# A third ready product at the change of stages, GpSimd's share of the statistics, and the row sums of attention on VectorE

## The chip, the cores and the metric

The kernel runs on one core of a Trainium2 chip. The metric is the device time of one execution in microseconds (us). The engines are named in full here; in rows of the profile PE is TensorE, DVE VectorE, ACT ScalarE, POOL GpSimd and SP SyncE, which issues most transfers.

## What is computed

One layer for 2048 tokens of 1024 channels in fp32: a normalization, one wide projection, a pooling branch and a causal stick-breaking attention branch, each with a SiLU gate path, merged by two sigmoid gates, projected out, added to the input and normalized again.

```python
h = rms_norm(x, norm_g)
u_pool, z_pool, q, k, v, z_attn, gate_logits = split(h @ w_in)
y_pool = multiscale_pool(u_pool, pool_w, pool_scale) * silu(z_pool)   # causal means of 2, 4, 8, 16
log_beta     = log_sigmoid(q @ k.T / 8)                               # 8 heads of 64
log_1m_beta  = where(s < t, log_sigmoid(-logits), 0)
later        = reversed_cumsum(log_1m_beta) - log_1m_beta
attn         = where(s < t, exp(log_beta + later), 0) @ v
y_attn = attn * silu(z_attn)
gates  = sigmoid(gate_logits + b_gate)
x = x + (gates[0] * (y_pool @ w_pool_up) + gates[1] * (y_attn @ w_attn_up)) @ w_out
out = rms_norm(x, final_g)
```

## The kernel before

**Products.** Every fp32 product is made of three matmuls on operands split into a high part, rounded to fp32r, and a low remainder (split3, L75 to L77, in the attention stage L1870 to L1874). ScalarE writes the high part ("hi"), GpSimd or VectorE the low one. The large projections go by seven products in place of eight: of the 2 x 2 blocks of a group the products A11, A12, S2, S1, S3, S4 and A22 are formed. These seven are the "parts" of a group, of 12 matmuls of 128x512 each; a part with sums needs an operand that VectorE or GpSimd forms (raw_forms and form_low on the side of the tokens, w_formed on the side of the weights). The results of a group come from sums of parts: ScalarE takes A11, S2 and S1 out of PSUM (take, L1027 in the front, L1983 in attention), VectorE adds A12, S3 and S4 (add_part, L2069), and the four results (A12, S3, S4, A22) are split or activated and stored.

**Three blocks of code.** `front` computes the statistics of the tokens, the normalized and transposed tokens hT, the value projection of 16 token tiles (project_v, L1352 to L1371) and 12 groups of projections, in two halves of 8 tiles and 6 groups. The second half overwrites tiles of the first, so the change of halves waits for stores. `stage3` is the attention stage: 8 heads of 40 items each (an item is up to 128x512 scores), with the remaining projections as filler matmuls between them. `stage4` computes the up projections, gates, output and last normalization. Between the blocks all engines meet at a barrier, and SyncE comes to it when the last stores of the block are done.

**The front.** Each engine's program is written out by hand in the order of slots `s`; PART_AT says which part a slot holds, and functions such as results_at, pooling_at_slot and splits_at say what else an engine does in it. The statistics of tokens go in batches: ScalarE sums squares (square, L951), VectorE makes the mean and its reciprocal (mean, L1149, L1151), ScalarE the square root (root, L956), VectorE refines it to the factors (factors, L1159 to L1165), ScalarE puts a tile's factors on a diagonal (make_diag, L962), TensorE spreads that over the partitions (spread, L1340, into PSUM), and VectorE scales the transposed tokens by it (scale, L1182, eight instructions). ScalarE then rounds them (tile_high, L987) and GpSimd makes the low part (tile_low, through the helper at L871). results_at gives the slot in which the results of a part are split and stored (result_high, L1039); a result of K or Q goes through the tile front_store, which must have been stored before it is written again (SyncE issues the stores, L749). pooled_high (L1055) rounds the level sums of the pooling branch.

**The change of stages.** Two parts of the first group of stage 3 (A11, A12; READY_PARTS) are computed at the end of the front, so that TensorE has work while other engines come to the barrier. Behind it GpSimd fills the tile floor (L2160, L2162), for which VectorE waits before its first instruction.

**Attention.** The items of a head go through rows of 128 queries from the last to the first, and through 1 to 4 blocks of keys in each row. In a slot s ScalarE writes keep (a sigmoid of the scores, L1956), VectorE scans it (scan: L2042 for the first item of a row, L2045 for the others) into left, TensorE turns that (L1901), ScalarE rounds it to wt (L1963) and VectorE makes its low part (L2051), and TensorE multiplies by the values (L1913), with high and low parts of the values side by side. A row's end has four steps: ScalarE copies a half (half_sum, L1971), VectorE adds the other and the end term (add_halves, L2060, into row_sum), and GpSimd adds the two halves into y_out (finish_row, L2103), which VectorE must see done before it writes row_sum two rows on. There are 128 row ends. A head's last twelve items hold eight of them. GpSimd's other work there is the low parts and forms of weights (low_w). The fillers follow a table `due`, which is worked out from a cost per item and gives the number of matmuls that shall be done by each item; the ends of parts follow from it (fin, PART_END, RESULT), and the reload of the second half's forms (hT from form_scratch) from fin as well. A result k is activated by ScalarE (result), and for z strips multiplied by VectorE (silu, L2073); the result with k % 4 = 3 goes to sum_d, straight from PSUM, so that the filler behind it, which needs that bank, waits for it.

```python
fin = [-1] * READY_PARTS + [next(s for s in range(len(due)) if due[s] >= ends_at[r]) for r in range(READY_PARTS, PARTS)]
PART_END = [f + 1 for f in fin]
RESULT = [fin[result_part(k)] + 1 for k in range(RESULTS)]
```

## Time and profile before

| | |
|---|---|
| three runs | 1577.16, 1579.95, 1581.51 us; median 1579.95 |
| profiled execution | 1579.27 us |
| its span, first to last instruction | 1577.4 us |
| mean granted TensorE clock | 0.992 |
| HBM read, written | 166.80 MB, 85.99 MB (160 GB/s over the span) |

The busy shares stand in the first group of rows below. TensorE is busy nearly everywhere, so the profile is best read by what ends its idle times (the list of waits), by windows around them with the granted clock, and by the timelines of the engines that end them. Busy time of TensorE counts an instruction from its start to a modelled end, and neighbouring matmuls overlap.

### The profile page before, as it was taken

The page shows a single profiled execution, that of the slowest core. Times are in us where ns is not written, and L with a number is a line of the kernel's source. Part 1 is how long each engine was busy: PE and PEld are TensorE (multiplying, and loading weights), DVE is VectorE, ACT ScalarE, POOL GpSimd, SP SyncE. Part 2 cuts the span into 40 slices and gives each one's busy share as a digit, 9 for nine tenths or more (in the row PEclk, how much of TensorE's full clock was granted, in tenths as well). Part 3 has the DMA queues.
Part 4 walks back from the last instruction along what each step waited for, and adds up shares of the span by engine and source line. Part 5 has one row for each costly group of instructions (what it writes and reads, how often), then busy time and mean ns, then how long its engine had stood idle before and what let it go on. Part 6 is the DMA issues. An engine that isn't in the chain of part 4 may idle for free. (4 is left out here: it accounts for less than half of the span.)

```text
span 1577.4 us, 24982 instructions
## 1 busy us (share of the span) xinstructions
PE 1530.4 (97%) x7770; PEld 1275.2 (81%) x7770; DVE 1237.2 (78%) x1592; ACT 856.2 (54%) x1653; POOL 1102.0 (70%) x770
## 2 busy tenths in 40 slices
PE   7999999998999999999998999999999999999998
PEld 5787878886888887888877888888888788888886
DVE  7968595766987788887897887798878656687987
ACT  6546554444666665666665676666766512233342
POOL 4899876985977678777766776787756334456774
PEclk9999999999999999999999999999999999999999
DMA  7468942465344343343694442443423688764552
GB/s 270 151 240 310 376 125 92 118 214 169 87 109 112 89 127 102 94 139 93 185 329 143 129 120 87 120 114 99 121 71 83 209 272 257 251 197 166 181 190 110
DMA packets 170803, 254.45 MB, mean 161 GB/s; under 512 B 48417, under 2 KB 82209, under 8 KB 170674
## 3 DMA queue, kind: packets, MB, share of 16 engines
q1 hardware_dynamic: 170674, 252.85, 51.2%
q8 instruction: 66, 1.08, 0.3%
q14 instruction: 63, 0.52, 0.1%
HBM read 166.80 MB, written 85.99 MB: 160 GB/s over the span
## 5 line engine op out<-in xcount | busy, mean ns | idle before, releaser
L2103 POOL TENSOR_TENSOR ring<-raw,ring 128x512 fp32r<-128x512 f32 x140 | 241.2, 1723 | 154.3 <-ACT ring L1950 143.9
L2045 DVE TENSOR_TENSOR_SCAN left<-keep,left 128x512 f32<-128x512 f32 x192 | 283.8, 1478 | 61.9 <-issue 40.1
L1870 PE MATMUL psum<-hT,ring 128*128 128x512 f32 x664 | 273.9, 412 | 14.7 <-ACT sum_a L1983 5.1
L1874 PE MATMUL psum<-hT,ring 128*128 128x512 f32 x664 | 271.8, 409 | 0.0
L1872 PE MATMUL psum<-hT,ring 128*128 128x512 f32 x664 | 271.2, 408 | 0.0
L1956 ACT ACTIVATE keep<-psum 128x512 f32<-128x512 f32 (+3 forms) x320 | 170.8, 534 | 131.8 <-PE psum L1893 119.2
L1963 ACT ACTIVATE wt<-psum 128x512 fp32r<-128x512 f32 (+3 forms) x320 | 171.0, 534 | 111.3 <-PE psum L1901 108.6
L2051 DVE TENSOR_TENSOR wt<-psum,wt 128x512 fp32r<-128x512 f32 (+3 forms) x320 | 190.3, 595 | 16.5 <-ACT wt L1963 13.9
L1913 PEld LDWEIGHTS psum<-wt,vm 128*128 128x128 f32 x1088 | 171.6, 189 | 26.9 <-DVE wt L2051 1.5
L1913 PE MATMUL psum<-wt,vm 128*128 128x256 f32 x1088 | 181.5, 281 | 1.0 <-DVE wt L2051 1.0
L1901 PE MATMUL psum<-ident,left 128*128 128x128 f32 x1088 | 171.1, 272 | 4.0 <-DVE wt L2051 4.0
L1901 PEld LDWEIGHTS psum<-ident,left 128*128 128x128 f32 x1088 | 137.2, 141 | 44.7 <-DVE left L2042 2.7
L2042 DVE TENSOR_TENSOR_SCAN left<-keep,floor 128x512 f32<-128x512 f32 (+3 forms) x128 | 134.7, 1052 | 32.4 <-ACT keep L1956 30.6
L1870 PEld LDWEIGHTS psum<-hT,ring 128*128 128x128 f32 x664 | 126.3, 190 | 37.1 <-DVE sum_d L2073 6.3
L1874 PEld LDWEIGHTS psum<-hT,ring 128*128 128x128 f32 x664 | 126.2, 190 | 18.6
L1872 PEld LDWEIGHTS psum<-hT,ring 128*128 128x128 f32 x664 | 126.4, 190 | 17.6
L871 POOL TENSOR_TENSOR ring<-raw,ring 128x512 fp32r<-128x512 f32 x76 | 120.9, 1591 | 27.6 <-ACT ring L1049 18.6
L75 PE MATMUL psum<-hT,ring 128*128 128x512 f32 x344 | 134.6, 391 | 3.4 <-POOL ring L871 1.5
L77 PE MATMUL psum<-hT,ring 128*128 128x512 f32 x344 | 134.1, 390 | 0.0
L76 PE MATMUL psum<-hT,ring 128*128 128x512 f32 x344 | 134.1, 390 | 0.0
L2103 POOL TENSOR_TENSOR y_out<-row_sum 64x128 f32<-64x128 f32 x128 | 101.0, 789 | 42.8 <-DVE row_sum L2060 27.9
L1892 PE MATMUL psum<-km,qm 128*128 128x512 f32 (+3 forms) x320 | 116.2, 363 | 2.9 <-DMA qm<-qk_scratch 2.1
(262 smaller groups left out, 3410.1 us busy)
## 6 DMA issues: line engine op xcount, KB each, us to landing
raw<-in_w_strips SPq DMA_DIRECT2D x144, 256.0 KB, 4.0
qm<-qk_scratch SPq DMA_DIRECT2D x128, 128.0 KB, 4.5
gate<-gate_scratch SPq DMA_DIRECT2D x64, 256.0 KB, 4.7
form_scratch<-hT SPq DMA_DIRECT2D x28, 512.0 KB, 7.0
hT<-form_scratch SPq DMA_DIRECT2D x28, 512.0 KB, 8.3
km<-qk_scratch SPq DMA_DIRECT2D x64, 128.0 KB, 3.7
merged_scratch<-rows SPq DMA_DIRECT2D x32, 256.0 KB, 5.0
mt<-merged_scratch SPq DMA_DIRECT2D x16, 512.0 KB, 5.8
```

The costliest lines, as they stand in the source:

```text
L75: pe.matmul(out, w_hi, m_hi, start=start, stop=False, skip_group_check=onto)
L1870: pe.matmul(o, hi, m_hi, start=k == 0 and not onto, stop=False, skip_group_check=onto)
L1872: pe.matmul(o, hi, m_lo, start=False, stop=False, skip_group_check=onto)
L1874: last = pe.matmul(o, lo, m_hi, start=False, stop=k == HK - 1, skip_group_check=onto)
L1901: last = pe.transpose(bank_t(n)[:, j * P:(j + 1) * P], left[:, n % LN, a:a + P], ident[:, :])
L1913: last = pe.matmul(bank_o(row), vm[:, t % VN, j, :], wt[:, n % WN, j, :, :].rearrange("p a q -> p (a q)"), start=first and j == 0, stop=fi ...
L1956: act.activation(keep[:, n % 2, CH - w:CH], bank_s(n)[:, 0:w], ACT.Sigmoid, scale=-SCALE).then_inc(keep_done, 1)
L1963: act.activation(wt[:, n % WN, 0:w // P, 0, :], bank_t(n)[:, 0:w].rearrange("p (j q) -> p j q", q=P), ACT.Copy).then_inc(wt_hi_done, 1)
L2042: dve.tensor_tensor_scan(left[:, n % LN, span][:, ::-1], k, floor[:, span][:, ::-1], carry, ALU.mult, ALU.max).then_inc(scanned, 1)
L2045: dve.tensor_tensor_scan(left[:, n % LN, span][:, ::-1], k, k, carry, ALU.mult, ALU.bypass).then_inc(scanned, 1)
L2051: dve.tensor_tensor(wt[:, n % WN, 0:w // P, 1, :], bank_t(n)[:, 0:w].rearrange("p (j q) -> p j q", q=P), wt[:, n % WN, 0:w // P, 0, :].bit ...
L2103: pool.tensor_tensor(out_, a, b, op).then_inc(s, 1)
```

## The change

1. `READY_PARTS` goes from 2 to 3. The front computes a third product (S2) of stage 3's first group, and ScalarE takes A11's product there, into a tile `ready_sum` that is handed to stage 3 as sum_a. Stage 3's fillers begin with S1, and 1980 matmuls of them are left of 1992, so that the table `due` gives other steps.
2. The factors of batches 2, 3, 4 and 5 are worked out by GpSimd. VectorE's mean(4) moves from before the loop of slots into tile_step(2), ScalarE's rounding of tile 2 moves ahead of root(3), and mean(b) waits for the factors of the batch before.
3. In results_at the last group of either half (groups 5 and 11) has its results one slot sooner; before, this held for the very last part alone. pooled_high comes one slot later, and there ahead of the splits.
4. In attention VectorE does finish_row, behind the scan of the same slot, and GpSimd no longer does. ScalarE's and VectorE's part of every fourth result comes ahead of the keep, or the row's end and scan, of its slot.

Calls that only pass `ready_sum` on, and the assertion that results stay in order, are left out here.

```diff
@@ -273,8 +273,9 @@
         head_loads = HeadLoads(sem, heads, qk_d, v_d)
+        ready_sum = heads("sum_a", [P, CH])[:, :]
         front(nc, sem, psum, at, free_at, hT_at, ident, ident_r, gcol, bcol, pscol, v_ends, hT, ring, raws, staging, ring_at, raw1_at,
-              x, x_T, norm_gT, w_v, b_gateT, pool_scaleT, w_strips, pool_w, pool_fix, v_d, qk_d, mix_d, form_d, head_loads)
+              x, x_T, norm_gT, w_v, b_gateT, pool_scaleT, w_strips, pool_w, pool_fix, v_d, qk_d, mix_d, form_d, head_loads, ready_sum)
...
@@ -295,7 +296,7 @@
 FRONT_PARTS = FRONT_GROUPS * FORMS
-READY_PARTS = 2
+READY_PARTS = 3
 RING_AT = FRONT_PARTS % RING
...
@@ -548,8 +549,8 @@
         lagged = [PART_AT.get(s - 2), PART_AT.get(s - 1)]
-        at_slot = [r for r, last in zip(lagged, (False, True))
-                   if r is not None and r < FRONT_PARTS and (r == FRONT_PARTS - 1) == last]
+        at_slot = [r for r, soon in zip(lagged, (False, True))
+                   if r is not None and r < FRONT_PARTS and (r // FORMS % HALF_GROUPS == HALF_GROUPS - 1) == soon]
         return [(r // FORMS, r % FORMS) for r in at_slot if not is_u(r // FORMS) and r % FORMS in OUT_PARTS]
...
@@ -891,6 +892,22 @@
+            def factors(b):
+                tiles = range(*BATCHES[b])
+                pool.wait_ge(rooted, b + 1)
+                for n in tiles:
+                    last = pool.tensor_scalar(stat[:, 4, n:n + 1], stat[:, 3, n:n + 1], stat[:, 3, n:n + 1],
+                                              stat[:, 1, n:n + 1], ALU.mult, ALU.mult)
+                last.then_inc(statistics, 1)
+                pool.wait_ge(statistics, 5 * b + 3)
+                part = stat[:, 5, tiles.start:tiles.stop]
+                pool.tensor_scalar(part, stat[:, 4, tiles.start:tiles.stop], -0.5, 1.5, ALU.mult, ALU.add).then_inc(statistics, 1)
+                pool.wait_ge(statistics, 5 * b + 4)
+                for n in tiles:
+                    last = pool.tensor_scalar(stat[:, 6, n:n + 1], stat[:, 5, n:n + 1], stat[:, 3, n:n + 1], 1.0,
+                                              ALU.mult, ALU.mult)
+                last.then_inc(statistics, 1)
+
...
@@ -909,6 +926,10 @@
                 i = n % FRONT_TILES
+                if n == 2:
+                    factors(4)
+                if batch_at(n) is not None:
+                    factors(batch_at(n))
                 if i in (3, 5):
...
@@ -926,7 +947,9 @@
                      wv_lo_pool, i - WV // 2 + 1)
+            factors(2)
             tile_low(1)
+            factors(3)
             for s in range(SLOTS):
...
@@ -1001,7 +1024,8 @@
                 i = n % FRONT_TILES
-                tile_high(n)
+                if n != 2:
+                    tile_high(n)
                 if later(n):
...
@@ -1024,7 +1048,10 @@
                     act.wait_ge(summed, 3 * (g - 1) + FRONT_ADD[S3 if j == A11 else S4])
-                act.activation(sum_u if j == S2 else sum_a, bank(g, j), ACT.Copy).then_inc(taken, 1)
+                if g == FRONT_GROUPS:
+                    act.wait_ge(mixed, 2 * MIXED_FIRST)
+                act.activation(ready_sum if g == FRONT_GROUPS else sum_u if j == S2 else sum_a, bank(g, j), ACT.Copy
+                               ).then_inc(taken, 1)
...
@@ -1085,6 +1112,7 @@
             square(3)
+            tile_high(2)
             root(3)
...
@@ -1092,7 +1120,7 @@
                 r = PART_AT.get(s - 1)
-                if r is not None and r < FRONT_PARTS:
+                if r is not None and r <= FRONT_PARTS:
                     g, j = divmod(r, FORMS)
...
@@ -1106,6 +1134,9 @@
                     copy_v(n - 2)
+                for f, q, step in pooling_at_slot(s):
+                    if step == LEVELS[q] + 2:
+                        pooled_high(f, q)
                 for w in splits_at(s):
...
@@ -1117,9 +1148,6 @@
                         mix_weights_high(f)
-                for f, q, step in pooling_at_slot(s):
-                    if step == LEVELS[q] + 1:
-                        pooled_high(f, q)
                 for f, q in mixes_at(s - 1):
...
@@ -1145,6 +1173,8 @@
                 tiles = slice(*BATCHES[b])
+                if b:
+                    dve.wait_ge(statistics, 5 * b)
                 dve.wait_ge(squared, BATCHES[b][1])
...
@@ -1153,7 +1183,7 @@
                 dve.wait_ge(rooted, b + 1)
-                if tiles.stop - tiles.start <= 2:
+                if tiles.stop - tiles.start == 1:
                     root_of = [stat[:, 3, n:n + 1] for n in range(tiles.start, tiles.stop)]
...
@@ -1209,7 +1239,9 @@
                 i = n % FRONT_TILES
-                if n != 2:
+                if n == 2:
+                    mean(4)
+                else:
                     scale(n)
...
@@ -1218,7 +1250,6 @@
                     mean(batch_at(n))
-                    factors(batch_at(n))
...
@@ -1289,13 +1320,9 @@
             mean(2)
-            factors(2)
             first_forms(0)
             mean(3)
-            factors(3)
             scale(2)
-            mean(4)
-            factors(4)
             for s in range(SLOTS + 2):
...
@@ -2001,13 +2029,17 @@
             act.sem_inc(w_hi_done, RING)
+            act.sem_inc(taken, 1)
             for s in range(-9, END):
...
                     for j in TAKE:
-                        if s == PART_END[part(g, j)]:
+                        if s == PART_END[part(g, j)] and part(g, j) > 0:
                             take(g, j)
+                for k in at(RESULT, s):
+                    if k % 4 == 3:
+                        result(k)
                 if 0 <= s < ALL:
...
@@ -2018,7 +2050,8 @@
                 for k in at(RESULT, s):
-                    result(k)
+                    if k % 4 < 3:
+                        result(k)
                 if ALL - 4 <= s < ALL:
...
@@ -2060,6 +2093,16 @@
+            def finish_row(n):
+                e, i, row = item(n)[0], item(n)[1], row_of(n)
+                mine = slice(e * HD, e * HD + HD)
+                u = row // 4
+                dve.wait_ge(row_done, row + 1)
+                if i % 4 == 3:
+                    wait(dve, y_stored[u % 2], u // 2, DMA)
+                dve.tensor_tensor(y_out[mine, u % 2, i % 4 * P:i % 4 * P + P], row_sum[mine, row % 2, 0:P],
+                                  row_sum[mine, row % 2, P:2 * P], ALU.add).then_inc(y_done, 1)
+
...
@@ -2080,12 +2123,17 @@
                             add_part(g, j)
+                for k in at(RESULT, s):
+                    if kind(k // 4) < 2 and k % 4 == 3:
+                        silu(k)
                 if s - AV_LAG - 1 in LAST:
...
                     scan(s)
+                if s - AV_LAG - 1 in LAST:
+                    finish_row(s - AV_LAG - 1)
                 for k in at(RESULT, s):
-                    if kind(k // 4) < 2:
+                    if kind(k // 4) < 2 and k % 4 < 3:
                         silu(k)
...
@@ -2121,16 +2169,6 @@
-            def finish_row(n):
-                e, i, row = item(n)[0], item(n)[1], row_of(n)
-                mine = slice(e * HD, e * HD + HD)
-                u = row // 4
-                pool.wait_ge(row_done, row + 1)
-                if i % 4 == 3:
-                    wait(pool, y_stored[u % 2], u // 2, DMA)
-                step(y_out[mine, u % 2, i % 4 * P:i % 4 * P + P], row_sum[mine, row % 2, 0:P],
-                     row_sum[mine, row % 2, P:2 * P], ALU.add, y_done, row + 1)
-
...
@@ -2171,8 +2209,6 @@
                         value_lo(u)
-                if s - AV_LAG - 1 in LAST:
-                    finish_row(s - AV_LAG - 1)
                 for k in at(RESULT, s):
...
                         times_mix(k)
```

**ScalarE at the start of the front.** The names: stat holds the statistics (L956 root, before; L979 after), diag the diagonals, xt_ring and xt_first the tokens whose squares are summed, hT<-xT the rounding of a tile. Before:

```order
L956 ACTIVATE stat<-stat 128x1 [waits f_statistics]
L962 ACTIVATE diag<-ident,stat 128x128 [waits f_spread,f_statistics]
L951 ACTIVATE xt_first,stat<-xt_first 128x1024 [waits f_x_in0]
L951 ACTIVATE xt_first,stat<-xt_first 128x1024 [waits f_x_in1]
L956 ACTIVATE stat<-stat 128x2 [waits f_statistics]
L987 ACTIVATE hT<-xT 128x4x128 [waits f_scaled] x2
L962 ACTIVATE diag<-ident,stat 128x128 [waits f_spread,f_statistics]
L951 ACTIVATE xt_ring,stat<-xt_ring 128x1024 [waits f_x_in2]
```

and with the change:

```order
L1010 ACTIVATE hT<-xT 128x4x128 [waits f_scaled] x2
L979 ACTIVATE stat<-stat 128x1 [waits f_statistics]
L985 ACTIVATE diag<-ident,stat 128x128 [waits f_spread,f_statistics]
L974 ACTIVATE xt_first,stat<-xt_first 128x1024 [waits f_x_in0]
L974 ACTIVATE xt_first,stat<-xt_first 128x1024 [waits f_x_in1]
L979 ACTIVATE stat<-stat 128x2 [waits f_statistics]
L985 ACTIVATE diag<-ident,stat 128x128 [waits f_spread,f_statistics]
L974 ACTIVATE xt_ring,stat<-xt_ring 128x1024 [waits f_x_in2]
```

The two roundings of tile 2 stood behind two squares and a root; now they stand ahead of root(3), and the diagonal, the squares and root(4) behind them.

**ScalarE at the change of halves**, in the last group of the first half. front_store<-... is the high part of a result, wv_hi a split of the value weights for the second half, front_sum_u and front_sum_a takes, ring the high part of filler weights. Before:

```order
L1039 ACTIVATE front_store<-psum 128x512 [waits f_out_lo,f_hi_stored2,f_part]
L970 ACTIVATE wv_hi<-wv_raw 128x1024 [waits f_wv_in1]
L1049 ACTIVATE ring<-raw_6_65 128x512 [waits f_part,f_block_in1]
L970 ACTIVATE wv_hi<-wv_raw 128x1024 [waits f_wv_in2]
L1027 ACTIVATE front_sum_u<-psum 128x512 [waits f_summed,f_part]
L1049 ACTIVATE ring<-raw_0_58 128x512 [waits f_part,f_block_in0]
L1039 ACTIVATE front_store<-front_out_d 128x512 [waits f_out_lo,f_hi_stored0,f_summed]
L970 ACTIVATE wv_hi<-wv_raw 128x1024 [waits f_wv_in3]
L962 ACTIVATE diag<-ident,stat 128x128 [waits f_spread,f_statistics] x2
```

and with the change:

```order
L1066 ACTIVATE front_store<-psum 128x512 [waits f_out_lo,f_hi_stored2,f_part]
L993 ACTIVATE wv_hi<-wv_raw 128x1024 [waits f_wv_in1]
L1076 ACTIVATE ring<-raw_6_65 128x512 [waits f_part,f_block_in1]
L1066 ACTIVATE front_store<-front_out_d 128x512 [waits f_out_lo,f_hi_stored0,f_summed]
L993 ACTIVATE wv_hi<-wv_raw 128x1024 [waits f_wv_in2]
L1053 ACTIVATE front_sum_u<-psum 128x512 [waits f_summed,f_part]
L1076 ACTIVATE ring<-raw_0_58 128x512 [waits f_part,f_block_in0]
L993 ACTIVATE wv_hi<-wv_raw 128x1024 [waits f_wv_in3]
L985 ACTIVATE diag<-ident,stat 128x128 [waits f_spread,f_statistics] x2
```

The result from front_out_d stands three places sooner and ahead of the take of front_sum_u.

**VectorE at two row ends of attention.** left is written by the scans, wt by the low parts, row_sum by add_halves. Before:

```order
L2060 SCALAR_TENSOR_TENSOR row_sum<-psum,v_ends,half_sum 64x256 [waits s3_y,s3_half]
L2042 SCALAR_TENSOR_TENSOR left<-keep,floor 128x128 [waits s3_turned,s3_keep]
L2051 TENSOR_TENSOR wt<-psum,wt 128x2x128 [waits s3_wt_hi]
L2045 SCALAR_TENSOR_TENSOR left<-keep,left 128x512 [waits s3_turned,s3_keep,s3_scanned]
L2051 TENSOR_TENSOR wt<-psum,wt 128x4x128 [waits s3_wt_hi]
L2060 SCALAR_TENSOR_TENSOR row_sum<-psum,v_ends,half_sum 64x256 [waits s3_y,s3_half]
```

and with the change:

```order
L2093 SCALAR_TENSOR_TENSOR row_sum<-psum,v_ends,half_sum 64x256 [waits s3_y,s3_half]
L2075 SCALAR_TENSOR_TENSOR left<-keep,floor 128x128 [waits s3_turned,s3_keep]
L2103 TENSOR_TENSOR y_out<-row_sum 64x128 [waits s3_y_stored0,s3_row]
L2084 TENSOR_TENSOR wt<-psum,wt 128x2x128 [waits s3_wt_hi]
L2078 SCALAR_TENSOR_TENSOR left<-keep,left 128x512 [waits s3_turned,s3_keep,s3_scanned]
L2084 TENSOR_TENSOR wt<-psum,wt 128x4x128 [waits s3_wt_hi]
L2093 SCALAR_TENSOR_TENSOR row_sum<-psum,v_ends,half_sum 64x256 [waits s3_y,s3_half]
```

Between the scan and the low part behind it VectorE now adds the row's halves into y_out.

## Rows read from the trace of the kernel before

**Rows 1.** The page, part 1: busy us, share of span, instructions by engine.

```profile
PE 1530.4 (97%) x7770; PEld 1275.2 (81%) x7770; DVE 1237.2 (78%) x1592; ACT 856.2 (54%) x1653; POOL 1102.0 (70%) x770
```

**Rows 2.** TensorE's waits: line, what ended them, total us, times, longest.

```profile
PE psum L1870 <- ACT sum_a L1983: 5.1, 1, 5.1
PE psum L1870 <- DVE sum_d L2073: 4.2, 4, 1.7
PE psum L1901 <- DVE wt L2051: 4.0, 4, 2.3
PE psum L1870 <- DMA hT<-form_scratch: 3.9, 1, 3.9
PE psum L1352 <- ACT hT L987: 2.7, 1, 2.7
PE psum L75 <- ACT front_sum_u L1027: 1.4, 1, 1.4
```

**Rows 3.** Windows: stretch, length, TensorE busy (instructions), granted clock, DMA share, GB/s.

```profile
25.00:30.00 5.00, 2.20 (x7) 0.74 0.26 107
373.40:376.00 2.60, 2.57 (x6) 0.50 0.41 101
834.40:838.00 3.60, 3.60 (x11) 0.50 1.03 337
607.00:612.00 5.00, 2.72 (x16) 1.00 0.02 3
```

**Rows 4.** Timeline (start, us), TensorE, end of the front; 35 alike between.

```profile
359.81 0.39 PE L77 MATMUL psum<-hT,ring 128*128 128x512 f32 x1
...
367.97 0.39 PE L77 MATMUL psum<-hT,ring 128*128 128x512 f32 x1
```

**Rows 5.** Timelines, start of the front; in brackets idle before, releaser.

```profile
27.68 1.13 ACT L987 ACTIVATE hT<-xT 128x512 fp32r<-128x512 f32 x2
...
30.22 0.63 PE L1340 MATMUL psum<-diag,ones 128*128 128x128 f32 x2
...
35.92 1.19 PE L1352 MATMUL psum<-wv_hi,b 128*128 128x512 f32 x4 [0.69 <-ACT b L987]
```

**Rows 6.** Timelines of ScalarE and TensorE, around the change of halves.

```profile
181.36 0.60 ACT L1027 ACTIVATE front_sum_u<-psum 128x512 f32<-128x512 f32 x1 [1.08 <-PE psum L77]
...
183.88 0.39 PE L75 MATMUL psum<-hT,ring 128*128 128x512 f32 x1
...
185.29 0.63 ACT L1039 ACTIVATE front_store<-front_out_d 128x512 fp32r<-128x512 f32 x1 [2.82 <-issue]
...
199.49 1.16 PE L1352 MATMUL psum<-wv_hi,b 128*128 128x512 f32 x4 [1.87 <-ACT b L987]
```

**Rows 7.** Timelines of GpSimd and VectorE, at the change of stages.

```profile
372.77 0.52 POOL L2160 MEMSET floor<- 128x512 f32 x1 [7.74 <-POOLq L682]
...
373.76 0.69 DVE L2069 TENSOR_TENSOR sum_b<-psum,sum_a 128x512 f32<-128x512 f32 x1 [5.55 <-POOL floor L2162]
```

**Rows 8.** Groups by line in the attention stage (VectorE), and the page's of GpSimd.

```profile
L2045 DVE TENSOR_TENSOR_SCAN left<-keep,left 128x512 f32<-128x512 f32 x192 | 283.8, 1478 | 61.9 <-issue 40.1 <-ACT keep L1956 20.1 <-PE psum L1901 0.7
...
L2060 DVE SCALAR_TENSOR_TENSOR row_sum<-psum,v_ends,half_sum 64x256 f32<-64x256 f32 x128 | 61.5, 481 | 25.1 <-POOL y_out L2103 11.9 <-ACT half_sum L1971 11.4
...
L2073 DVE TENSOR_TENSOR sum_b<-sum_b,staging 128x512 f32<-128x512 f32 x8 | 11.6, 1445 | 1.8 <-ACT staging L1998 1.7
...
L2103 POOL TENSOR_TENSOR y_out<-row_sum 64x128 f32<-64x128 f32 x128 | 101.0, 789 | 42.8 <-DVE row_sum L2060 27.9
```

**Rows 9.** Timeline of VectorE, an add of 128x256 from SBUF in the front.

```profile
341.81 0.42 DVE L123 TENSOR_TENSOR v_raw<-v_prev,v_raw 128x256 f32<-128x256 f32 x1
```

**Rows 10.** Windows of all engines, sum over the eight stretches with eight row ends.

```profile
sum 216.80, PE 213.85 PEld 182.61 DVE 183.25 ACT 154.32 POOL 149.50; mean PE 26.73 PEld 22.83 DVE 22.91 ACT 19.29 POOL 18.69
```

**Rows 11.** Timelines of VectorE and TensorE, a scan and the matmuls that turn it.

```profile
480.19 0.69 DVE L2042 TENSOR_TENSOR_SCAN left<-keep,floor 128x256 f32<-128x256 f32 x1 [0.42 <-ACT keep L1956]
...
483.52 0.38 PE L1901 MATMUL psum<-ident,left 128*128 128x128 f32 x2
```

9 lines of the change are left out of this document (5 added, 4 removed).

## Prediction

> **What bounds the kernel now.** I read the share of each engine first. The profiled execution took 1579.27 us. TensorE is busy 97% of the span and VectorE 78% [rows 1], so time is won only where TensorE stands idle or runs at half its clock, and lost where something new stops it. TensorE's list of waits names the places that the change touches [rows 2]: 5.1 us for ScalarE's first sum of the attention stage (the change of stages), 4.2 us for the SiLU of sum_d, 4.0 us for wt, 3.9 us for a reloaded form, 2.7 us for hT at the start, 1.4 us for front_sum_u. The windows add what an idle costs behind it [rows 3]: after the idle of 5.1 us the granted clock was 0.50 (1.2 GHz, against 1.00 for 2.4 GHz), it was 0.50 after the reload's 3.9 us, and it had begun to fall at the start, behind the 2.7 us. Behind the idle of 2.3 us at 607 it stayed at 1.00. From 359.81 to 367.97 TensorE goes 36 steps from one matmul to the next [rows 4], 0.227 us each, so 12 of them take 2.72 us. At the half clock 6 fill 2.57 us [rows 3], 0.43 each. A stay there as long as the reload's 3.6 us or more [rows 3] loses at least half of itself; from the durations between the two levels I take 2.7 to 3.4 us for a clock fall beyond the idle.
>
> **The start of the front.** The factors of statistics batches 2 to 5 go to GpSimd, and ScalarE rounds tile 2 before root(3), where it did so behind root(4). Removed: the wait for hT. That work ended at 28.8 and was queued behind two squares and a root [rows 5]; now it follows the scaling directly, and the first product can start near 27.6, 0.75 us sooner. Added: diag(3), the two squares, mean(4) and root(4) are all later by the 1.13 us rounding and the wait for its input. I place the squares' end at 29.5 and root(4) at 30.2. GpSimd's five small operations follow, each waiting for the one before. No row shows one on GpSimd; its fill of 128x512 took 0.52 us [rows 7], so each costs between nothing and 0.52. I take 0.34 with its hand-over, since one column is far less work than a fill: 1.7 us for five, so diag(4) is ready near 32.4. The spread matmul that stood at 30.22 without a wait [rows 5] then waits until there, TensorE's queue behind it. The next scaling follows, and the product that started at 35.92 starts near 37.8: +1.9, taken as **+2**. Bounds: −1 (the five at almost nothing, the start's clock kept) to +4.5 (0.52 us each and a longer stay at the half clock). Batches 2, 3 and 5 stay beside VectorE's scalings, which they relieve.
>
> **Pooled levels behind the takes.** pooled_high one slot later but ahead of the splits frees ScalarE for front_sum_u. The 1.4 us wait goes [rows 2]: **−1.4**.
>
> **The change of halves.** Group 5's results now come one slot sooner, so the result of S4 (front_store from front_out_d) stands ahead of a weight split and of the take of front_sum_u on ScalarE. The take began at 181.36; that result could only start at 185.29 after 2.82 us of waiting for a store to land [rows 6]. Now ScalarE stands from some 179.3 until that landing, which nothing makes earlier, and the split and the take follow it: the take at 186.6, done at 187.2. TensorE's part that needs the emptied bank began at 183.88 without a wait [rows 6]: a stall of 3.3 us. Of it 1.9 us come back, as the wait of 1.87 us at 199.49 for the next store's landing [rows 6] ends no later, and some 0.9 as the last results leave a slot sooner: +0.5. But 3.3 us lies above the 2.7 us behind which the clock fell [rows 3], which adds 2.7: **+3**. Bounds +0.5 and +3.2.
>
> **The change of stages.** TensorE ended at 368.36 [rows 4] and idled for 5.1 us, to 373.4 [rows 2]. ScalarE's take of A11, and GpSimd's fill of the floor, from 372.77, both stood behind the barrier, and VectorE's first add behind the floor [rows 7]. The barrier waits for the last results' stores. Now TensorE has 12 more matmuls, to 371.1 (2.72 us), and the last group's three other results leave one slot sooner, so I open the barrier 0.8 us sooner. The third part's A11 product is taken in the front; what then holds TensorE is VectorE's add of A12, behind the floor: 371.9 + 1.75 = 373.6. It restarts as late as before with 12 matmuls fewer to do: −2.7, +0.2: −2.5. The idle is 2.5 us in place of 5.1, in between 2.3 (no fall) and 2.7 (fall); without the fall another −2.6. I take half: **−3.8**, bounds −1.7 (the barrier no sooner) and −5.1.
>
> **The attention stage.** Off GpSimd go 128 sums of a row's halves, 789 ns each, 101 us [rows 8]; onto VectorE come 128 of the same shape, 64x128 from SBUF. VectorE waited 11.9 us in row_sum for GpSimd's sums [rows 8]; TensorE's stall of 2.3 us, most of the 4.0 for wt, hangs on one of these. ScalarE's and VectorE's part of every fourth result moves ahead of the keep and scan of its slot: that is TensorE's wait for sum_d, 4.2 us [rows 2]. Together some 6 us can be won. What does a sum cost on VectorE? From adds of 128x512 (0.69) and 128x256 (0.42) [rows 7, 9] a line gives 0.28 at 128 columns. The SiLU products, which read SBUF twice, took 1.45 us into sum_b [rows 8], and scans of 512 average 1.48 [rows 8], their spread coming, as I read it, from GpSimd's products beside them. So a sum costs 0.28 to 1.45; I take 0.8, a little under the middle, as it is the shortest operation and GpSimd, now the idler, meets fewer of them: 102 us more on VectorE. The cover: one stretch of some 27 us in each of the eight heads has eight row ends; in these, VectorE is idle 33.6 of 216.8 us in all [rows 10]. 64 sums at 0.8 are 51 us; relief from GpSimd, a third less busy there, I put at 5 us over all scans. 51 − 34 − 5 = 12 us short, 1.5 per stretch, against a lead of 2.6 us from a scan (ended 480.88) to the matmul that turns it (483.52) [rows 11]. It is carried, with some 2 us of new small stalls: **−4**, bounds −6 and the rival below.
>
> The Trainium skill, page "SBUF — State Buffer", section "SBUF: two separate sides", speaks against this move: a VectorE operation with two SBUF inputs and a GpSimd one that reads SBUF exclude each other, and the loser waits for the other's whole instruction. By it a sum would cost up to 0.28 plus one GpSimd product of 1.7 us, and the stage would lose rather than gain; the products and scans here agree in kind.
>
> **The reload at 834.40.** The steps move by one part, and the form loads' issue moves some 1.5 us sooner, as GpSimd sheds sums ahead of its last use; but one index later by the due table. 3.9 us of idle and a clock fall stand there [rows 2, 3]. **−1**, bounds −7 (both gone) and +3.
>
> Sum: +2 −1.4 +3 −3.8 −4 −1 = −5.2: 1574.1 for the profiled execution. The median of the runs is 1579.95, 0.7 above it: **1574.7**.
>
> **The rivals.**
> *New waits in front, clock falling.* The start at +4.5, the halves at +3.2, the stage change at −2.5 with its clock fall kept, attention −2, the reload 0: +1.8, 1581.8. For it: each of the three idles lies near 2.7, and the spread matmul had no wait. Against: the start's price rests on operations that may be short. 0.24.
> *VectorE becomes the bound (slower).* The mechanism is the sum in the eight dense stretches at 1.2 us, midway from 0.94 (below) to the SiLU product's 1.45: 77 − 34 − 5 = 38 us short, 4.7 a stretch, 2.6 of it carried, 2.1 times 8 = +17 where I have −4: 1574.7 + 21 = 1596. It decides from a mean of (34 + 5 + 21)/64 = 0.94 us. Between 0.8 and this point the small stalls grow, and the time runs from 1575 to 1580. Against: GpSimd also loses 101 us of the work that would stand in the way. 0.14.
> *More of the idles vanish.* The start −1, halves +0.5, stage change −5.1, attention −5, reload −4, pooled −1.4: −16.0, 1564. For it: each clock fall is all or nothing. 0.15.
> *It does not do what it says.* If the barrier is opened by a store or by TensorE itself, the third product only fills the idle: that is in the stage change's bound of −1.7 (within my case, 1577).
>
> **How the numbers follow.** My forecast has 0.47, with 1570 to 1579 as its own range. About 0.3%, 4.7 us, can be told from no change: faster is below 1575.2. My case gives 0.34 faster and 0.13 the same; the first rival 0.18 the same and 0.06 slower; the second 0.14 slower; the third 0.15 faster. Faster 0.49, the same 0.31, slower 0.20. The range of 1564 to 1586 reaches to the third case and the first's slower half, and leaves out 0.2, above all the VectorE case.
>
> **What would show it.** The spread matmul at the start waiting for ScalarE's diag some 2 us, and the half clock beyond 34 us. The 1.4 us wait for front_sum_u gone from 142.75, and one of about 3 us on it near 187. At the change of stages an idle of 2.3 to 2.7 ended by VectorE's sum_b, with or without a clock of 0.50. In attention no wait for sum_d above 0.5 us, y_out on VectorE near 0.8 mean, VectorE's sum up by 80 to 110 us, no rise in waits for wt. Wrong it would be if y_out averaged over 1 us and waits for wt grew to 10 us or more, or if the halves cost nothing.

## The result, and the profile after

The changed kernel's median is 1587.23 us (1584.94 to 1589.43, five runs), against 1579.95 for the kernel before (1575.48 to 1581.51). The ratio of the runs is 1.0059, with a 95% interval of 1.0042 to 1.0076. So it is slower, by 7.3 us in the medians and 9.3 by that ratio, where 5 us less were forecast, and it lies outside the range given (1564 to 1586). The profiled execution took 1584.94 us, with a span of 1583.2 us, 5.7 us over the profiled one of before.

TensorE's waits in the changed kernel, in the form of [rows 2]:

```profile
PE psum L1929 <- DVE wt L2084: 12.2, 16, 5.3
PE psum L1367 <- ACT diag L985: 6.0, 3, 3.0
PE psum L75 <- ACT front_sum_u L1053: 3.3, 1, 3.3
PE psum L1898 <- DVE sum_b L2112: 3.0, 1, 3.0
PE psum L1898 <- DMA hT<-form_scratch: 2.7, 2, 2.1
PE psum L1920 <- issue: 2.6, 1, 2.6
PE psum L1898 <- DVE sum_c L2112: 2.5, 2, 1.5
```

The waits of 5.1 us for sum_a, 4.2 us for sum_d, 2.7 us for hT and 1.4 us for front_sum_u are gone, and the one for the reloaded form fell from 3.9 to 2.7 us. In their place stand 6.0 us for the diagonals, 3.3 us for another front_sum_u, 3.0 us for sum_b and, the largest, 12.2 us for wt (5.0 before), with one wait of 5.3 us in it that nothing in the prediction foresaw. All engines over the attention stage (from:to, length, then busy us and instructions of TensorE, its weight loads, VectorE, ScalarE and GpSimd, then clock, DMA share and GB/s), before and after:

```profile
379.00:1240.00 861.00, 843.30 (x4801) 717.27 (x4801) 720.13 (x874) 570.50 (x1133) 629.17 (x458) 1.00 0.43 123
```

```profile
379.00:1240.00 861.00, 840.39 (x4774) 713.62 (x4773) 807.00 (x989) 564.38 (x1124) 553.96 (x331) 0.99 0.42 123
```

VectorE went from 84% to 94% busy there, GpSimd from 73% to 64%.

Where the time went is read best from the same instruction of TensorE in both timelines: its start in the kernel before, and how much later it starts in the changed one (and in three kernels of the next section). Product matmuls of the front are those of L75 to L77. Each column is one execution.

| place | before, us | changed | results alone (e6) | results and row sums (e4) | losses undone (e8) |
|---|---|---|---|---|---|
| 301st product matmul of the front | 138.5 | +2.3 | −0.3 | −0.1 | −0.1 |
| 421st | 167.6 | +0.7 | −2.0 | −1.8 | −1.8 |
| 41st of the second half's values | 205.3 | +3.9 | −1.4 | −1.1 | −0.8 |
| first matmul of scores | 378.7 | +3.4 | −1.1 | −1.4 | −0.7 |
| 17th of scores | 397.9 | +9.1 | −1.3 | −1.4 | +0.8 |
| last of scores | 1230.2 | +4.9 | −6.5 | −2.4 | −2.0 |
| end of the span | 1577.4 | +5.7 | −5.2 | −0.9 | −2.1 |

Behind the 205.3 the changed kernel's lag settles at +3.6 from about 213 to the end of the front. Later figures for other kernels are read in the same way: a lag is the distance from the kernel before at the same instruction. The part behind the 17th scores differs between executions of the same attention code: the kernels e6 and e12 below gain 5.3 and 9.5 us there, the changed kernel, e1 and e2 4.2, 3.5 and 0.3, and e3 loses 0.6.

**Start.** ScalarE, TensorE and GpSimd of the changed kernel, which answer to [rows 5]:

```profile
27.10 0.40 ACT L985 ACTIVATE diag<-ident,stat 128x128 f32<-128x128 f32 x1 [1.12 <-POOL stat L907]
...
32.60 0.40 ACT L985 ACTIVATE diag<-ident,stat 128x128 f32<-128x128 f32 x1 [2.31 <-POOL stat L907]
...
30.40 1.29 POOL L899 TENSOR_SCALAR stat<-stat 128x1 f32<-128x1 f32 x2 [0.68 <-ACT stat L979]
31.78 0.19 POOL L904 TENSOR_SCALAR stat<-stat 128x2 f32<-128x2 f32 x1
32.07 0.49 POOL L907 TENSOR_SCALAR stat<-stat 128x1 f32<-128x1 f32 x2
...
27.56 0.80 PE L1367 MATMUL psum<-diag,ones 128*128 128x128 f32 x2 [2.39 <-ACT diag L985]
...
33.05 0.80 PE L1367 MATMUL psum<-diag,ones 128*128 128x128 f32 x2 [2.99 <-ACT diag L985]
```

GpSimd's five operations take 2.2 us, and diag(4) starts at 32.60. TensorE waits twice, for diag(3) and for diag(4), with its clock at 0.50 from 26.9 to 37.1 us, where it was 27.4 to 34.2 before.

**The change of halves.** In the form of [rows 6]:

```profile
185.91 0.63 ACT L1066 ACTIVATE front_store<-front_out_d 128x512 fp32r<-128x512 f32 x1 [5.91 <-DMA qk_scratch<-front_store]
186.45 1.04 ACT L993 ACTIVATE wv_hi<-wv_raw 128x1024 fp32r<-128x1024 f32 x1
187.39 0.58 ACT L1053 ACTIVATE front_sum_u<-psum 128x512 f32<-128x512 f32 x1
...
188.02 0.79 PE L75 MATMUL psum<-hT,ring 128*128 128x512 f32 x1 [3.31 <-ACT front_sum_u L1053]
```

ScalarE stands 5.9 us for a store to land, and what is queued behind it reaches TensorE as a stall of 3.3 us. (The row of before, in [rows 6], put its 2.82 us down to "issue"; this one names the store.) The window behind it shows the half clock, as do windows behind the change of stages, the opening of attention and the reload:

```profile
188.00:191.00 3.00, 2.98 (x7) 0.50 1.04 412
378.30:381.60 3.30, 3.30 (x10) 0.52 0.33 85
395.80:398.60 2.80, 2.80 (x11) 0.50 0.41 89
842.50:845.80 3.30, 3.30 (x13) 0.53 1.04 323
```

**The change of stages.** GpSimd, VectorE and TensorE, in the form of [rows 7]:

```profile
375.88 0.53 POOL L2198 MEMSET floor<- 128x512 f32 x1 [6.90 <-POOLq L683]
...
376.88 0.69 DVE L2112 TENSOR_TENSOR sum_b<-psum,sum_a 128x512 f32<-128x512 f32 x1 [5.53 <-POOL floor L2200]
...
377.62 0.50 PE L1898 MATMUL psum<-hT,ring 128*128 128x512 f32 x1 [2.96 <-DVE sum_b L2112]
```

TensorE now waits 2.96 us for VectorE's add, which stands behind the floor.

**The opening of attention.** Here the largest single loss arises. ScalarE, GpSimd, VectorE and TensorE of the changed kernel:

```profile
386.79 0.61 ACT L1984 ACTIVATE keep<-psum 128x512 f32<-128x512 f32 x1
391.72 0.63 ACT L1978 ACTIVATE ring<-second 128x512 fp32r<-128x512 f32 x1 [4.33 <-POOL second L2151]
392.25 0.58 ACT L1991 ACTIVATE wt<-psum 128x512 fp32r<-128x512 f32 x1
392.73 0.62 ACT L2026 ACTIVATE staging<-sum_c 128x512 f32<-128x512 f32 x1
...
389.62 2.06 POOL L2151 TENSOR_TENSOR second<-raw,raw 128x512 f32<-128x512 f32 x1
...
393.38 1.60 DVE L2116 TENSOR_TENSOR sum_c<-sum_c,staging 128x512 f32<-128x512 f32 x1 [2.75 <-ACT staging L2026]
394.91 0.68 DVE L2084 TENSOR_TENSOR wt<-psum,wt 128x512 fp32r<-128x512 f32 x1
...
395.74 1.09 PE L1929 MATMUL psum<-ident,left 128*128 128x128 f32 x4 [5.29 <-DVE wt L2084]
```

and ScalarE in the kernel before:

```profile
384.50 0.62 ACT L1963 ACTIVATE wt<-psum 128x512 fp32r<-128x512 f32 x1
...
390.67 0.62 ACT L1950 ACTIVATE ring<-second 128x512 fp32r<-128x512 f32 x1
391.31 0.60 ACT L1963 ACTIVATE wt<-psum 128x512 fp32r<-128x512 f32 x1
```

`second` is the S2 operand of the second filler group, which GpSimd forms behind two low parts and another form. Its split by ScalarE (ring<-second) stood ahead of the fourth wt before, and met an operand that was ready; now it stands ahead of the first. With a third product taken out of the stage, TensorE is 12 matmuls further on at the same item, the parts end at earlier items, and the split moves with them: ScalarE comes to it 4.3 us too early, and the first wt, at 384.50 before, waits until 392.25 behind it.

**Row sums.** y_out in the changed kernel (count, duration ns min/median/max), VectorE's groups of the attention stage in the form of [rows 8], and the sum over the eight stretches with eight row ends in the form of [rows 10]:

```profile
L2103 DVE TENSOR_TENSOR y_out<-row_sum x128: 254/760/1365, 409.1 to 1246.5; 64x128 f32<-64x128 f32 x128
```

```profile
L2078 DVE TENSOR_TENSOR_SCAN left<-keep,left 128x512 f32<-128x512 f32 x192 | 282.9, 1473 | 18.7 <-issue 12.3 <-ACT keep L1984 5.3 <-PE psum L1929 0.2
...
L2103 DVE TENSOR_TENSOR y_out<-row_sum 64x128 f32<-64x128 f32 x128 | 104.6, 817 | 2.0
```

```profile
sum 216.80, PE 213.01 PEld 180.99 DVE 206.60 ACT 150.39 POOL 120.82; mean PE 26.63 PEld 22.62 DVE 25.83 ACT 18.80 POOL 15.10
```

A sum costs 0.82 us, as estimated, and VectorE is left with 10 us of idle in 217 us where it had 34. The scans of this line average 1473 ns where they had 1478, but the two kernels differ in more than the sums; e4 and e6 below compare them alone.

### The profile page after: what moved, and what is told of

Its sections match the earlier page's. It is cut to its first block and busy times, and to the rows that moved or that the text cites. A ratio compares the mean times of both kernels' runs of the same rounds, so it can differ in the third digit from the quotient of the medians.

```text
span 1583.2 us, 24892 instructions
## 1 busy us (share of the span) xinstructions
PE 1533.0 (97%) x7770; PEld 1276.5 (81%) x7770; DVE 1321.9 (84%) x1704; ACT 854.6 (54%) x1653; POOL 1032.1 (65%) x658
## 5 line engine op out<-in xcount | busy, mean ns | idle before, releaser
L2151 POOL TENSOR_TENSOR ring<-raw,ring 128x512 fp32r<-128x512 f32 x140 | 251.0, 1793 | 236.5 <-ACT ring L1978 231.0
L2078 DVE TENSOR_TENSOR_SCAN left<-keep,left 128x512 f32<-128x512 f32 x192 | 282.9, 1473 | 18.7 <-issue 12.3
L1929 PE MATMUL psum<-ident,left 128*128 128x128 f32 x1088 | 171.8, 273 | 12.3 <-DVE wt L2084 12.2
L2075 DVE TENSOR_TENSOR_SCAN left<-keep,floor 128x512 f32<-128x512 f32 (+3 forms) x128 | 145.1, 1134 | 13.9 <-ACT keep L1984 12.2
L75 PE MATMUL psum<-hT,ring 128*128 128x512 f32 x348 | 137.3, 395 | 5.0 <-ACT front_sum_u L1053 3.3
L872 POOL TENSOR_TENSOR ring<-raw,ring 128x512 fp32r<-128x512 f32 x76 | 119.7, 1574 | 28.6 <-ACT ring L1076 19.3
L77 PE MATMUL psum<-hT,ring 128*128 128x512 f32 x348 | 136.6, 393 | 0.0
L1920 PE MATMUL psum<-km,qm 128*128 128x512 f32 (+3 forms) x320 | 116.4, 364 | 3.1 <-issue 2.6
L1921 PE MATMUL psum<-km,qm 128*128 128x512 f32 (+3 forms) x320 | 117.1, 366 | 0.0
```

Source lines behind the costliest of these rows:

```text
L75: pe.matmul(out, w_hi, m_hi, start=start, stop=False, skip_group_check=onto)
L77: return pe.matmul(out, w_lo, m_hi, start=False, stop=stop, skip_group_check=onto)
L1929: last = pe.transpose(bank_t(n)[:, j * P:(j + 1) * P], left[:, n % LN, a:a + P], ident[:, :])
L2078: dve.tensor_tensor_scan(left[:, n % LN, span][:, ::-1], k, k, carry, ALU.mult, ALU.bypass).then_inc(scanned, 1)
L2151: pool.tensor_tensor(out_, a, b, op).then_inc(s, 1)
```

## The experiments

Twelve kernels ran, five executions or more each. The medians of the kernel before beside them were 1579.2 to 1580.0 us. The interval of one kernel's ratio is some 2 us to either side, so a difference between two of them is uncertain by about 3 us, and the timelines of the profiled runs are read beside them. Gains over the changed kernel are given by the medians; by the ratios to the kernel before they are up to 2 us larger, as the changed kernel's own loss is (9.3 in place of 7.3).

**e1: the statistics as before.** From the changed kernel, GpSimd's factors are taken out and ScalarE's order at the start is put back:

```diff
             square(3)
-            tile_high(2)
             root(3)
...
             mean(2)
+            factors(2)
             first_forms(0)
             mean(3)
+            factors(3)
             scale(2)
+            mean(4)
+            factors(4)
```

> The changed kernel with the statistics as they were (factors on VectorE, the rounding of tile 2 behind root(4)). Theory 1 (each order puts a wait of its own on TensorE): the two waits for ScalarE's diag, 2.4 and 3.0 us near 27.5 and 33, go, one of 2.7 us for hT comes back, and the product behind stands 2.6 us sooner; later gaps keep their size, so the time is some 2 to 3 us under the changed kernel's. Rival (the start's loss is swallowed by a later wait for a store): the offset at the change of halves is the same as in the changed kernel, and the time stays within 1 us of it.

Measured: 1584.18 us (1582.52 to 1589.58), 3.0 us under the changed kernel. The two waits for diag are gone; the 2.75 us for hT is back, and the first scores stand 2.6 us sooner than in the changed kernel. That is so although this execution lost 1.8 us to the very first diagonal, at 8.8 us, which the change does not touch. Theory 1 holds for the start, with a size at the limit of what the runs can tell.

**e2: the results of group 5 in their old slots.**

```diff
-                   if r is not None and r < FRONT_PARTS and (r // FORMS % HALF_GROUPS == HALF_GROUPS - 1) == soon]
+                   if r is not None and r < FRONT_PARTS and (r // FORMS == FRONT_GROUPS - 1) == soon]
```

> The changed kernel with the results of group 5 in their old slots (those of the last group, 11, stay one slot sooner). Theory 1: ScalarE's take of front_sum_u no longer stands behind the result from front_out_d, so TensorE's wait of 3.3 us near 188 and the half clock of 6.8 us behind it go, the wait of about 1.9 us for b near 200 comes back, and everything behind is 2.9 us sooner: time 2 to 4 us under the changed kernel's. Rival: the old order would wait for the same landing in another place, and nothing is won.

Measured: 1585.98 us (1585.38 to 1588.68), 1.3 us under the changed kernel, less than the 2 to 4 expected and within the uncertainty. In the trace the wait for front_sum_u is gone, one of 2.82 us for b at 201.24 is in its place, and the first scores stand 1.9 us sooner (+1.4 against +3.4). From the 421st product of the front to its end this execution loses 0.6 us where the changed kernel loses 2.9. In the traces of all kernels the old order loses 0.6 to 1.2 us there (e2, e4, e6 to e8, e11, e12) and the new one 1.5 to 3.7 (the changed kernel, e1, e3, e5, e9, e10). So the new order costs, some 2 us, and a part of what pooled_high had gained is waited off in either order, here with 2.82 us for b in place of 1.87.

**e3: wt ahead of the splits in the first ten slots.**

```diff
+                if 0 <= s - T_LAG < 8:
+                    high_part(s - T_LAG)
                 for w in at(W_STEP, s):
                     split_w(w)
-                if 0 <= s - T_LAG < ALL:
+                if 8 <= s - T_LAG < ALL:
                     high_part(s - T_LAG)
```

> The changed kernel, but in the first ten slots of attention ScalarE rounds wt before it splits filler weights. Theory 2 (with three ready products ScalarE's split of the S2 operand comes ahead of the first wt and waits 4.3 us there for GpSimd to form it, and wt, VectorE's low part and TensorE's turn are queued behind): TensorE's stall of 5.3 us near 396 and the half clock near 395 to 399 go or shrink below 1.5 us, offset at the end of attention and time 4 to 6 us less. Rival (VectorE is too busy with what it took over): its order is not touched, so the stall stays above 4 us and the time within 1.5 us.

Measured: 1584.28 us (1582.89 to 1591.99; the profiled execution is the slowest, 1591.99), 3.0 us under the changed kernel. The stall at the opening shrank only from 5.3 to 3.9 us, and from the first to the 17th scores this kernel loses 5.6 us, as much as the changed one (5.7). Theory 2 in this form fell, its rival (a stall above 4 us, the time within 1.5) did not come out either, and no trace locates the 3 us. The trace does say why the stall stayed. ScalarE and VectorE of this kernel:

```profile
387.66 0.61 ACT L1991 ACTIVATE wt<-psum 128x512 fp32r<-128x512 f32 x1
392.12 0.63 ACT L1978 ACTIVATE ring<-second 128x512 fp32r<-128x512 f32 x1 [3.84 <-POOL second L2153]
392.65 0.61 ACT L2026 ACTIVATE staging<-sum_c 128x512 f32<-128x512 f32 x1
...
393.30 0.74 DVE L2118 TENSOR_TENSOR sum_c<-sum_c,staging 128x512 f32<-128x512 f32 x1 [2.27 <-ACT staging L2026]
393.96 0.68 DVE L2086 TENSOR_TENSOR wt<-psum,wt 128x512 fp32r<-128x512 f32 x1
```

wt's high part is early now, at 387.66, but VectorE's low part stands behind the SiLU of sum_c, whose sigmoid (staging) still stands behind ring<-second on ScalarE. The wait was taken out of one of two paths.

**e5: the split itself two slots later.** This takes both away.

```diff
     def split_step(w):
-        return fin[freed(w)] + 1 if w >= RING else -99
+        return fin[freed(w)] + (3 if freed(w) == 4 else 1) if w >= RING else -99
```

> The changed kernel, but the split of the tenth filler part's weights (S2 of the second group, whose operand GpSimd forms at the opening) two slots later, so that neither wt nor the sigmoid for sum_c stands behind ScalarE's wait for it. Theory 2b (the opening's stall is ScalarE's wait for the formed operand, and what is queued behind it on ScalarE and VectorE): the stall of 5.3 us near 396 falls under 1.5 us, no half clock there, and the sixteenth item stands 5 to 6 us sooner against the first than in the changed kernel; time 1580 to 1583. Rival (GpSimd's low parts or VectorE's load are late in any order): the stall stays above 3.5 us, the time above 1584.

Measured: 1583.50 us (1576.86 to 1588.94), 3.7 us under the changed kernel. ScalarE, VectorE and TensorE:

```profile
388.79 0.61 ACT L1991 ACTIVATE wt<-psum 128x512 fp32r<-128x512 f32 x1
...
392.08 1.68 DVE L2116 TENSOR_TENSOR sum_c<-sum_c,staging 128x512 f32<-128x512 f32 x1
393.68 0.68 DVE L2084 TENSOR_TENSOR wt<-psum,wt 128x512 fp32r<-128x512 f32 x1
...
394.51 0.87 PE L1929 MATMUL psum<-ident,left 128*128 128x128 f32 x3 [2.53 <-DVE wt L2084]
```

ScalarE no longer waits ahead of wt, but 2.5 us of the stall are left: VectorE has three scans, two SiLU products and an add ahead of the first low part, where the kernel before had three scans and one SiLU product (its second came at 393.72, behind three low parts). The add and the second product take 2.3 us. So theory 2b accounts for 2.8 of the 5.3 us, and the rest, as I read it, is work of VectorE that the third product pulls into the filling of the pipeline. The rival was right about that rest; neither side's figure for the stall (under 1.5, above 3.5) came out. From the first to the 17th scores the loss is 3.2 us here and 1.5 in e8, which has the same edit, against 5.7 in the changed kernel; with the stall of 5.3 us unchanged it is 6.9 in e1, 6.0 in e2 and 7.0 in e9, where the clock stands at 0.50 for 6.8 us in place of 3.4.

**e10: two ready products.** All else as changed:

```diff
-READY_PARTS = 3
+READY_PARTS = 2
...
-                if r is not None and r <= FRONT_PARTS:
+                if r is not None and r < FRONT_PARTS:
...
-            act.sem_inc(taken, 1)
...
-                        if s == PART_END[part(g, j)] and part(g, j) > 0:
+                        if s == PART_END[part(g, j)]:
```

> The changed kernel with two ready products as before, all else as changed. Theory 2: the opening's stall of 5.3 us and its half clock go, 12 matmuls (2.7 us) come back into the stage and the idle at the change of stages grows by 2 us: 1583 to 1586. If the third product is worth what it was meant to be (an idle filled, no other cost): 1589 or more.

Measured: 1579.98 us (1577.78 to 1583.08), 7.3 us under the changed kernel, more than the 1 to 4 expected. The idle at the change of stages is 4.56 us in place of 2.96, the 12 matmuls are back, and still the last scores stand 5.0 us sooner (−0.1 against +4.9). There is no stall of more than 0.9 us at the opening, and from the first to the 17th scores nothing is lost (−0.2): one constant makes the opening's loss come and go. The third ready product cost as much as the whole change lost, 7.3 us in the medians; that is more than its stall of 5.3 us. By the two profiled executions it is 4.6 us from the front's end to the last scores, and what lies between that and the 7.3 was not located.

**e4, e6, e7: the two moves in attention, apart and together.** All three take the front, the statistics and the two ready products of the kernel before, and keep pooled_high behind the takes. e4 has both moves. e6 has the order of every fourth result alone:

```diff
+                for k in at(RESULT, s):
+                    if k % 4 == 3:
+                        result(k)
                 if 0 <= s < ALL:
                     remaining(s)
...
                 for k in at(RESULT, s):
-                    result(k)
+                    if k % 4 < 3:
+                        result(k)
...
+                for k in at(RESULT, s):
+                    if kind(k // 4) < 2 and k % 4 == 3:
+                        silu(k)
                 if s - AV_LAG - 1 in LAST:
                     add_halves(s - AV_LAG - 1)
...
                 for k in at(RESULT, s):
-                    if kind(k // 4) < 2:
+                    if kind(k // 4) < 2 and k % 4 < 3:
                         silu(k)
```

and e7 has the row sums alone (GpSimd's finish_row goes):

```diff
                 if s < ALL:
                     scan(s)
+                if s - AV_LAG - 1 in LAST:
+                    finish_row(s - AV_LAG - 1)
```

> The kernel before with only the attention part of the change (row sums on VectorE, every fourth result ahead of the keep and scan) and pooled_high behind the takes; two ready products, statistics and results of the front as before. Theory 1 and 2 (the losses lie in the front and at the opening of attention, the moves in attention win): no stall for wt above 2 us at the opening, attention 2 to 5 us shorter than before, time 3 to 6 us under the kernel before. Rival (VectorE is the bound with sums of 0.82 us): waits for wt and sum_c grow to 7 us or more as in the changed kernel, attention is as long as before or longer, time within 1.5 us of before or over it.

> The kernel before with every fourth result ahead of the keep and scan and pooled_high behind the takes, row sums on GpSimd as before. Theory 3 (the order of the results wins, the move of the row sums gives back what it wins): waits for sum_d under 1 us in all in place of 4.2, the 2.3 us wait behind GpSimd's row sum stays; time 2 to 4 us under the kernel before, and at least as low as with the row sums on VectorE (1577.5). Rival (the row sums' move carries the gain): time within 1.5 us of before.

> The kernel before with the row sums on VectorE and pooled_high behind the takes, results in their old order. Theory 3: a sum costs 0.8 us, waits for wt grow by 3 us or more over the 4.0 of before, the 4.2 us for sum_d stay; time between that of before and 3 us over it, or at best 1 us under it for pooled_high. Rival: waits for wt do not grow, the 2.3 us one goes, and the time is 2 us or more under before.

| kernel | results early | row sums | median, us | ratio, 95% interval |
|---|---|---|---|---|
| e6 | yes | GpSimd | 1570.61 | 0.9941 (0.9925 to 0.9958) |
| e4 | yes | VectorE | 1577.45 | 0.9983 (0.9971 to 0.9994) |
| e7 | no | VectorE | 1590.02 | 1.0068 (1.0055 to 1.0082) |

The order of results is worth 9 us with pooled_high's 1.7, and the row sums take 7 of them back (e4 against e6); without the order they cost 11 (e7 against before). The two are not independent: with the row sums on VectorE and the results late, the waits for sum_d do not stay at 4.2 us but grow to 7.1, with one of 3.1. Theory 3 holds, and more strongly than expected: e7 lies 11 us over before where at most 3 was expected, and e6 beat its expected 2 to 4 us. e4 lies between its two cases: the waits grew as the rival said, and the time is 2.5 us under before, where theory had 3 to 6 and the rival 1.5 or less. TensorE's waits, e6, then e4:

```profile
PE psum L1906 <- DVE wt L2060: 4.0, 4, 2.2
PE psum L1918 <- DVE wt L2060: 1.0, 1, 1.0
```

```profile
PE psum L1906 <- DVE wt L2060: 6.1, 11, 1.0
PE psum L1918 <- DVE wt L2060: 3.5, 2, 1.8
```

The eight stretches with eight row ends, e6, then e4:

```profile
sum 216.80, PE 213.80 PEld 182.61 DVE 184.63 ACT 152.21 POOL 148.99; mean PE 26.73 PEld 22.83 DVE 23.08 ACT 19.03 POOL 18.62
```

```profile
sum 216.80, PE 213.63 PEld 181.69 DVE 209.13 ACT 152.87 POOL 115.89; mean PE 26.70 PEld 22.71 DVE 26.14 ACT 19.11 POOL 14.49
```

VectorE stands at 96% in e4's. The waits for wt grow from 5.0 us in 5 places to 9.6 us in 13. The scans do get shorter: all 320 of them take 417.7 us in e4 and 427.4 in e6, and 428.0 in the changed kernel against 442.9 in e9, which has the row sums back on GpSimd. So GpSimd's relief is there, 10 to 15 us, and it does not keep TensorE from waiting more.

**e9: the changed kernel with the row sums back on GpSimd.** Its edit is e7's taken back, with finish_row in GpSimd's loop as before.

> The changed kernel with the row sums on GpSimd as before, all else as changed. Theory 3 (the row sums on VectorE are the largest loss, 7 to 10 us, and hide the gain of the results' order): 1578 to 1581, waits for wt beside the opening's under 3 us, none for sum_c above 0.5. Rival (with three ready products the opening decides, and the row sums cost little there): 1584 or more.

Measured: 1581.95 us (1578.85 to 1583.62), 5.3 us under the changed kernel and just above the expected 1578 to 1581. The opening's stall stays at 5.28 us, and behind it one wait of 0.93 us for wt and one of 0.74 us for sum_c are left. This confirms e4 against e6 from the other side, and the stall at the opening does not come from the row sums.

**e11: a spare sum.** e6's kernel, and on VectorE a sum that nobody needs, into a tile of its own:

```diff
+            def spare_sum(n):
+                e, row = item(n)[0], row_of(n)
+                mine = slice(e * HD, e * HD + HD)
+                dve.wait_ge(row_done, row + 1)
+                dve.tensor_tensor(spare[mine, :], row_sum[mine, row % 2, 0:P - 8],
+                                  row_sum[mine, row % 2, P:2 * P - 8], ALU.add)
...
                 if s < ALL:
                     scan(s)
+                if s - AV_LAG - 1 in LAST:
+                    spare_sum(s - AV_LAG - 1)
```

> The kernel with only the order of results and pooled_high changed (1570.6), row sums on GpSimd, and beside them a spare sum on VectorE: 64x120 of the same two halves behind the same scans, written to a tile nobody reads. It leaves nothing out and adds 128 instructions. Theory 3a (it is VectorE's time that costs, in the dense stretches): the spare sum takes 0.7 to 1.0 us in the mean, TensorE's waits for wt grow as with the row sums there, and the time is 5 to 10 us over 1570.6. Rival (it is the new dependence, y_out's place ahead of the low part and the store's wait, that costs): within 2 us of 1570.6.

Measured: 1590.44 us (1588.61 to 1593.27), 19.8 us over e6. VectorE, GpSimd and the waits:

```profile
L2077 DVE TENSOR_TENSOR spare<-row_sum 64x120 f32<-64x120 f32 x125 | 99.2, 794 | 1.9
...
L2125 POOL TENSOR_TENSOR y_out<-row_sum 64x128 f32<-64x128 f32 x125 | 114.2, 914 | 43.9 <-DVE row_sum L2070 29.6 <-POOL ring L2125 1.5 <-POOL raw L2125 0.8
```

```profile
PE psum L1907 <- DVE wt L2061: 10.5, 12, 2.9
```

No result waits for this sum and no store holds it, so neither the dependence nor the store's wait is needed for a cost, as the rival had it; the place ahead of the low part is the same here, and a sum placed behind it was not tried. The expected 5 to 10 us were far too few. The cost need not be VectorE's time alone: GpSimd's own sum takes 914 ns here against 815 in e6, its products (ring) 1758 against 1718, VectorE's scans 1513 against 1488, and TensorE waits once, for 3.9 us, for GpSimd's vm; time on VectorE and the slowing of both engines were not told apart. With GpSimd's own sums kept beside it the price is 20 us where the move costs 7: by difference, what else the move does (above all the 101 us that GpSimd loses) would be worth some 13 us, an estimate.

**e8: the three losses undone.** The changed kernel with e1's, e2's and e5's edits together.

> The changed kernel with all three losses undone: statistics as before, group 5's results in their old slots, the tenth split two slots later; third ready product, pooled_high, the last group's results, results and row sums of attention as changed. If the ledger adds up (start 2.6, halves 2.9, opening 5.8 us less): 1574 to 1577. If the losses are not independent (a later wait swallows them, or the clock falls elsewhere): 1578 or more.

Measured: 1579.28 us (1576.98 to 1583.65), ratio 0.9999 (0.9988 to 1.0011). With the single gains of e1 (3.0), e2 (1.3) and e5 (3.7) the sum is 1587.3, against 1587.23 measured for the changed kernel: the three are independent as far as the runs can tell. Still the time fell into the case "1578 or more": 1574 to 1577 was added up from the timelines' 2.6, 2.9 and 5.8 us, and the edits gave back 8.0 in all, the opening above all less than its 5.8. Against e4, which has neither the third product nor the last group's results sooner, it is 1.8 us slower, within the uncertainty: even without ScalarE's wait no gain of the third product is seen.

**e12: the rounding of tile 2 between the two squares**, on e6's kernel.

```diff
-                tile_high(n)
+                if n != 2:
+                    tile_high(n)
...
             square(4)
+            tile_high(2)
             square(5)
```

> The kernel with only the order of results and pooled_high changed, and at the start ScalarE's rounding of tile 2 between the two squares that stood ahead of it (factors stay on VectorE). If the wait of 2.7 us for hT is only a matter of ScalarE's order: it shrinks to under 2 us, the spread of tile 4 waits less than 0.5 us, and the start is 0.7 to 1.5 us shorter: 1568 to 1570. If diag(4) is then late as in the changed kernel: a wait of 1 us or more for diag, and 1571 or more.

Measured: 1571.89 us (1569.01 to 1576.25), e6's time within the uncertainty, and the second case by both its signs. The wait for hT fell from 2.75 to 1.07 us, and a new one of 3.54 us for diag stands behind it. The 301st product of the front starts 2.6 us later than before, where the changed kernel has 2.3 and e6 −0.3. The diagonal of tile 4 was late in both orders tried in which this rounding comes ahead of root(4), with the factors on VectorE too. So the rounding's place by itself is enough for the changed kernel's loss at the start; whether GpSimd's factors add to it was not measured alone.

The fastest kernel of the study is e6, the order of results and pooled_high alone (e12 is within the uncertainty of it): 9.3 us under the kernel before by its ratio, and 16.6 under the changed one by the medians.

## Why the prediction was wrong

By its own steps, with the sizes from the timelines of the two profiled executions (a lag's growth over the step):

| step | forecast | measured |
|---|---|---|
| start | +2 | +2.3 |
| pooled_high | −1.4 | −1.7 |
| change of halves | +3 | +2.9 |
| change of stages, with the 12 matmuls | −3.8 | −2.9 |
| opening of attention | no term | +5.7 |
| attention behind it, and the reload | −4 −1 | −1.5 |
| stage 4 | no term | +0.8 |
| sum | −5.2 | +5.7 |

The change of stages is −0.2 from the lag at the first scores (+3.6 to +3.4) and −2.7 from the 12 matmuls. These are spread over the stage by the table of due counts: by TensorE's own records the changed kernel is 12 filler matmuls ahead at the first scores and still at the 17th, 7 ahead at the 257th and none at the last. From the 17th scores on the lag falls by 4.2 us, and 2.7 of it are these.

**Start, pooled_high, halves: right.** The spread matmul of tile 4 waited for the diagonal until 33.05 (forecast 32.4), GpSimd's five operations took 2.2 us (1.7), the take came at 187.39 (186.6) and the stall behind it was 3.3 us (3.3), with the half clock behind it. What I had not seen at the start is the second wait, 2.4 us for diag(3) at 27.56, ahead of the products that I placed at 27.6; but the product that I followed came at 38.53 where I had 37.8. That the change of halves came out at 2.9 is in part luck: the same order lost 1.5 to 3.7 us in six executions, and the old order 0.6 to 1.2 as well once pooled_high had moved.

**The change of stages: the mechanism right, the account closed too early.** The idle was 2.96 us where I had 2.5, ended by VectorE's sum_b behind the floor, with a short half clock behind it. The step that failed is that I took the 12 matmuls as won there: "It restarts as late as before with 12 matmuls fewer to do". I had compared the order of the engines' rows at three places, and the opening of attention was not among them. There the third product moves the split of `second` ahead of the first wt, and VectorE's results into the filling of the pipeline, and this stall of 5.3 us, 5.7 with its half clock, gave back twice what the 12 matmuls won. e10 puts the third product's net at +7.3 us in the medians (+4.6 in the timelines), e5 puts 3.7 of it on the split (2.5 in the timelines of the opening).

**The row sums: the price right, the cover wrong.** A sum was to cost 0.8 us and took 0.82; the other step that failed is "It is carried, with some 2 us of new small stalls". 12 us short over the eight stretches was the sum's own result; I set it against the lead of one scan as if that lead were spare in every stretch. The small waits for wt of e4 say that it was not, 9.6 us in 13 places where e6 has 5.0 in 5. The 5 us of relief that I gave for the scans did come, 10 us over all scans (e4 against e6), so it is not the term that failed. Measured price of the move: 7 us (e4 against e6), 5 (the changed kernel against e9). The rival with VectorE as the bound gave 1596 and put its start at a mean of 0.94 us. Its direction was right, its point of decision was not: at 0.82 already the sums cost several us.

**The results' order: right, and too small.** I summed the waits that it takes away, 4.2 us and a part of 1.2, and put 6 us on both moves together. e6 gains 9.3 us in all, of which 1.1 stand already at the first scores (pooled_high's 1.7 less what the stores take back), so some 8 by itself in the medians. Its waits for sum_d are gone. Its profiled execution, the slowest of its six, gains 5.3 us behind the 17th scores, near the waits' sum; e12's gains 9.5 with the same attention code. What divides the rest was not measured. With the order at some 8 and the row sums at 7, the two moves together are worth about 1 us (e4's lag from the first to the last scores, −1.0) where I had put −4.

The start and the halves by themselves were worth 3.0 and 1.3 us in the medians (e1, e2), near or below what I had given them, so the forecast's errors lie in the two steps above, and in the third product most of all.

## What to carry to other kernels

When a scheduler's table or a queue's order is shifted by one part, compare every engine's order at the next stage's opening, not only where the edit stands: an in-order engine that comes early to an operand that is not ready holds all that is queued behind it. Here an engine at 85% of a stretch had no free room for 10% more, though the operation was cheap and another engine was relieved; the lead of one engine over another is not idle time. And where a change bundles parts, measure them apart: here one part (the results' order, with pooled_high) was 9 us faster, and the whole 7 us slower.

## What the runs showed of the hardware

The prediction took 2.3 to 2.7 us of TensorE's idle as the line behind which the clock falls. The runs draw no such line: in the changed kernel it fell behind an idle of 2.11 us that ended at 841.68 (0.53 in the window above) and stayed at 1.00 behind one of 2.56 us that ended at 822.98; in the kernel before it stayed at 1.00 behind 2.28 us [rows 3], and in e4 it fell to 0.50 behind 1.81 us that ended at 721.41.

A sum of 64x128 with both operands in SBUF took from 254 to 1365 ns on VectorE, with a median of 760. The lower end is what a line through longer adds gave (0.28); the rest, as I read it, is waiting inside the instruction. GpSimd's products (ring) rose with the row sums on VectorE, from 1718 ns (e6) to 1813 ns (e4), and GpSimd's own sum from 815 (e6) to 914 ns (e11) beside the spare one; VectorE's scans became shorter as GpSimd's sums went (427.4 to 417.7 us in all, e6 to e4). The Trainium skill, page "SBUF — State Buffer", section "SBUF: two separate sides", says that a VectorE operation with two SBUF inputs and a GpSimd operation that reads SBUF hold a shared pair of ports in turn, each for its whole instruction; these numbers agree with it in kind, on both sides: the longest sum, 1365 ns, is 1.1 us above the shortest, less than one of GpSimd's products.
